# Routing logits taken from rows before their normalisation, and the order of loads around the first expert block

## The reference, cut to what matters

```
y = merged @ w_out
x = layer_norm(alpha * x + (1.0 + gt1) * y, ln_g[0], ln_b[0])
h = x * (1.0 + sc2) + sh2
p_grp  = softmax(h @ w_route_grp)             # 4 groups
logits = h @ w_route_exp                      # 32 experts, 8 in a group
# the best group, the two best experts in it, their gates
for each expert e:  hb = silu(xb @ w_gate[e]) * (xb @ w_up[e]);  yb = hb @ w_down[e]
x = layer_norm(alpha * x + (1.0 + gt2) * sum of gated yb, ln_g[1], ln_b[1])
```

## Time and profile before

| what | us |
|---|---|
| median of 3 runs (lowest, highest) | 2259.28 (2259.08, 2259.91) |
| the profiled execution's own time | 2261.59 |
| its span, first to last instruction | 2259.8 |
| TensorE busy | 2096.4 (93%) |
| VectorE busy | 1182.3 (52%) |
| ScalarE busy | 460.6 (20%) |

### The profile page before, as it was taken

One profiled execution on the slowest core, in us unless ns is written; L12 is line 12 of the kernel. 1 busy time (PEld: TensorE's weight loads), 2 busy tenths in 40 slices (PEclk: granted clock), 3 DMA queues, 4 the chain that ended last, 5 costly groups with the idle time before them and its releaser, 6 DMA issues.

```text
span 2259.8 us, 24654 instructions
## 1 busy us (share of the span) xinstructions
PE 2096.4 (93%) x9166; PEld 1344.4 (59%) x9166; DVE 1182.3 (52%) x2110; ACT 460.6 (20%) x948; POOL 132.2 (6%) x173
## 2 busy tenths in 40 slices
PE   8999898999999999998999999999996999999883
PEld 4444444888888845444788488888854433333331
DVE  2785654666677543367787467676446221121114
ACT  2215541100100010225211455410110000000003
POOL 1000000000000000000000043300000000010000
PEclk9999898999999999999999999999996999999996
DMA  7136600622122132221122000042445899999995
GB/s 260 61 118 239 221 1 1 158 75 90 60 103 103 56 100 75 75 75 38 38 75 88 24 2 1 2 152 75 168 168 233 348 423 426 426 427 426 426 401 221
DMA packets 97677, 364.71 MB, mean 161 GB/s; under 512 B 9340, under 2 KB 17969, under 8 KB 85521
## 3 DMA queue, kind: packets, MB, share of 16 engines
q1 hardware_dynamic: 88065, 340.62, 39.2%
q0 software_dynamic: 9392, 22.37, 2.8%
q10 hardware_dynamic: 96, 0.08, 0.0%
HBM read 357.00 MB, written 17.57 MB: 166 GB/s over the span
## 4 chain that ended last, share of the span: by engine, by line
PE 79%; DVE 12%; DMA 5%; issue 2%; ACT 2%; SPq 0%; DVEq 0%; ACTq 0%; POOLq 0%
PE bank L752 52%; PE bank L1552 9%; PE bank L1545 6%; PE bank L818 3%; DMA mem<-in_w_gate 2%; DMA mem<-in_w_up 2%; PE bank L1235 2%; PE bank L993 2%; PE bank L863 1%; PE bank L1526 1%; DVE mem L2166 1%; DVE mem L1669 1%; DVE mem L1664 1%; DVE mem L1668 1%; DVE mem L1665 1%
## 5 line engine op out<-in xcount | busy, mean ns | idle before, releaser
L752 PE MATMUL bank<-mem 128*128 128x256 f32 (+7 forms) x5032 | 1348.7, 430 | 24.1 <-ACT mem L2584 11.0
L752 PEld LDWEIGHTS bank<-mem 128*128 128x128 f32 (+2 forms) x5032 | 932.9, 192 | 392.2 <-issue 264.5
L1552 PE MATMUL bank<-mem 128*64 128x512 f32 x1184 | 269.3, 610 | 28.2 <-DMA mem<-in_w_gate 9.9
L1552 PEld LDWEIGHTS bank<-mem 128*64 128x64 f32 x1184 | 88.3, 140 | 198.9 <-issue 184.4
L2584 ACT ACTIVATE mem<-bank 128x512 f32<-128x512 f32 (+4 forms) x277 | 140.1, 506 | 325.0 <-PE bank L752 152.1
L818 PE MATMUL bank<-mem 128*128 128x128 f32 (+1 forms) x740 | 124.6, 302 | 39.1 <-DVE mem L1824 15.2
L2520 DVE TENSOR_TENSOR mem<-mem,bank 128x512 f32<-128x512 f32 x19 | 13.1, 690 | 268.6 <-PE bank L1552 171.0
L818 PEld LDWEIGHTS bank<-mem 128*128 128x128 f32 (+1 forms) x740 | 92.2, 152 | 95.3 <-DVE mem L1824 40.1
L1545 PE MATMUL bank<-mem 128*128 128x512 f32 x288 | 127.0, 596 | 4.1 <-ACT mem L2900 4.1
L2718 ACT ACTIVATE mem<-bank 128x512 f32<-128x512 f32 (+1 forms) x62 | 36.3, 585 | 459.8 <-PE bank L752 458.1
L1545 PEld LDWEIGHTS bank<-mem 128*128 128x128 f32 x288 | 53.5, 189 | 73.7 <-issue 68.4
(11 more groups left out here) (364 smaller groups left out, 1716.9 us busy)
## 6 DMA issues: line engine op xcount, KB each, us to landing
mem<-in_w_gate SPq DMA_DIRECT2D x37, 2048.0 KB, 23.3
mem<-in_w_up SPq DMA_DIRECT2D x35, 2048.0 KB, 25.2
mem<-in_w_down SPq DMA_DIRECT2D x34, 2048.0 KB, 26.7
mem<-in_w_in SPq DMA_DIRECT2D x18, 2048.0 KB, 8.0
mem<-in_w_ada SPq DMA_DIRECT2D x12, 2048.0 KB, 8.0
mem<-in_w_out SPq DMA_DIRECT2D x4, 2048.0 KB, 14.0
mem<-in_w_ple_gate SPq DMA_DIRECT2D x2, 2048.0 KB, 7.8
mem<-in_w_br_att SPq DMA_DIRECT2D x2, 2048.0 KB, 7.7
```

Source lines behind the costliest of these rows:

```text
L752: last = pe.matmul(o, l, r, start=(i == 0), stop=(i == len(pairs) - 1))
L1552: last_ = pe.matmul(o[here, :], lhs[:, k, here], w[:, k, cols], start=(k == 0), stop=(k == kk - 1))
```

## The change

Four things are changed, all between the mixer and the second expert block.

1. The rows are turned before they are normalised (`rows_turned`, as soon as `row_added` says that both halves are added), VectorE copies them plainly into `hT` (`rows_taken`), and the logits are made with weights that hold the gain and the scale (`w_by_row`, columns 0 to 35). A product of ones with `w_by_row` (`route_constants`, 72 columns) gives the sums that mean and shift need; `logits_taken` puts the two together in two small instructions, with the mean and the deviation that the normalisation has anyway. For this, gain and shift are loaded once more by column, and VectorE makes `w_by_row` before the output stage. The rows are still normalised and written to memory as before, but nothing of the logits waits for the long instructions.
2. The output products are taken by half tiles in a new order, with turns and logits products between them; two more small products stand ahead of the last one.
3. `all_slots` stands behind the gate product of block 0 and no longer in its middle; a gate product waits for the first half of its turned rows only, and in its middle for the second. The reduction into `place_of` stands behind the first `slots_from`.
4. Load 7 waits for the row writes, as load 8 does.

```diff
@@ -435,6 +435,9 @@
         flat_T = xgT.rearrange("p a b c -> p (a b c)")
+        route_rows, logit_sum = flat_T[:, 512:584], flat_T[:, 584:620]
+        w_by_row = place(M0 + 3 * D + KD * 36, KD, 72)
+        route_cols = choice_all[:, 0, 0, 0:2 * KD].rearrange("p (j k) -> p j k", j=2)
...
@@ -484,6 +487,7 @@
         x_spilled = sem("x_rows_written")
+        row_added = sem("out2_added_to_row")
...
@@ -1451,17 +1455,19 @@
 
-            def out2_rows(q):
-                for c in range(2):
-                    if q == 0 and c == 1:
-                        pe.wait_ge(fast_read, 5 * N_FAST)
-                    b = bank("dve")
-                    full(product(b[:, :], [(S5["mg"][:, k, q * P:(q + 1) * P], out2[c][:, k, :])
-                                           for k in range(KD)]), "dve")
-            def normal_rows_turned(q):
+            def out2_rows(q, c):
+                if q == 0 and c == 1:
+                    pe.wait_ge(fast_read, 5 * N_FAST)
+                b = bank("dve")
+                full(product(b[:, :], [(S5["mg"][:, k, q * P:(q + 1) * P], out2[c][:, k, :])
+                                       for k in range(KD)]), "dve")
+            def route_constants():
                 to_wait(to_pe)
-                mark["x normalised", q] = nxt[to_pe]
+                full(product(bank("dve")[:, 0:72], [(const("ones"), w_by_row[:, k, :]) for k in range(KD)]), "dve")
+            def rows_turned(q):
+                pe.wait_ge(row_added, q + 1)
...
@@ -1469,28 +1475,35 @@
                 pe.wait_ge(dve_free, turned_at[q])
-                full(product(b[:, 0:36], [(hT[:, k, q * P:(q + 1) * P], w_route[:, k, :]) for k in range(KD)]), "dve")
+                full(product(b[:, 0:36], [(hT[:, k, q * P:(q + 1) * P], w_by_row[:, k, 0:36]) for k in range(KD)]), "dve")
...
             assert done["dve"] % 4
-            out2_rows(0)
+            out2_rows(0, 0)
+            out2_rows(0, 1)
             pe.wait_ge(mixed_ready, 2)
-            out2_rows(1)
-            normal_rows_turned(0)
-            pe.wait_ge(route_loaded, 32)
-            out2_rows(2)
-            normal_rows_turned(1)
+            out2_rows(1, 0)
+            rows_turned(0)
+            out2_rows(1, 1)
+            out2_rows(2, 0)
+            rows_turned(1)
+            route_constants()
             routed_rows(0)
-            out2_rows(3)
+            out2_rows(2, 1)
+            out2_rows(3, 0)
+            rows_turned(2)
+            routed_rows(1)
+            out2_rows(3, 1)
...
             used("dve")
-            normal_rows_turned(2)
-            routed_rows(1)
             routed_rows(2)
-            normal_rows_turned(3)
-            mark["x normalised"] = nxt[to_pe]
+            rows_turned(3)
...
             routed_rows(3)
+            for q in range(NT):
+                nxt[to_pe] += 1
+                mark["x normalised", q] = nxt[to_pe]
+            mark["x normalised"] = nxt[to_pe]
...
@@ -1582,10 +1595,12 @@
 
-                pe.wait_ge(xt_taken, 2 * n + 2)
+                pe.wait_ge(xt_taken, 2 * n + 1)
...
                 expert_product(banks[2][:, :], xgT[:, n % 2, :, :], weights_here(n, "gate", wide_at), every, KD,
-                               all_slots if n == 0 else None).then_inc(gate_full, 1)
+                               lambda: pe.wait_ge(xt_taken, 2 * n + 2)).then_inc(gate_full, 1)
+                if n == 0:
+                    all_slots()
...
@@ -2364,6 +2379,12 @@
             V(dve.memset(ln_eps_col, LN_EPS))
+            dve.wait_ge(route_loaded, 64)
+            V(tt(route_cols, route_cols, mod[:, 3:4, :].to_broadcast([P, 2, KD]), ALU.mult))
+            V(tt(route_cols[:, 1, :], route_cols[:, 1, :], mod[:, 2, :], ALU.add))
+            for j in range(2):
+                V(tt(w_by_row[:, :, 36 * j:36 * j + 36], w_route, inner(route_cols[:, j, :], 36), ALU.mult),
+                  to_pe if j else None)
...
@@ -2374,39 +2395,48 @@
             dve.wait_ge(x_again, 16)
-            def out2_added(q):
-                for c in range(2):
-                    o = x[:, q, c * 512:(c + 1) * 512]
-                    V(tt(S5["tmp"], take()[:, :], gate_rows[:, 0, c * 512:(c + 1) * 512], ALU.mult), dve_free)
-                    V(stt(o, o, ALPHA, S5["tmp"], ALU.mult, ALU.add), var_ready if c else None)
+            def out2_added(q, c):
+                o = x[:, q, c * 512:(c + 1) * 512]
+                V(tt(S5["tmp"], take()[:, :], gate_rows[:, 0, c * 512:(c + 1) * 512], ALU.mult), dve_free)
+                V(stt(o, o, ALPHA, S5["tmp"], ALU.mult, ALU.add), row_added if c else None)
...
 
+            def rows_taken(q):
+                for hf in range(2):
+                    V(dve.tensor_copy(hT[:, 4 * hf:4 * hf + 4, q * P:(q + 1) * P],
+                                      take()[:, :].rearrange("p (a b) -> p a b", a=4)), dve_free)
             def logits_taken(q):
-                V(dve.tensor_copy(logit[:, q, :], take()[:, 0:36]), dve_free)
+                V(stt(logit_sum, route_rows[:, 0:36], stat[:, q:q + 1], take()[:, 0:36], ALU.mult, ALU.add), dve_free)
+                V(stt(logit[:, q, :], logit_sum, stat[:, 4 + q:5 + q], route_rows[:, 36:72], ALU.mult, ALU.add))
...
             V(dve.memset(both_and_none[:, NT, :], 0.0))
-            out2_added(0)
+            out2_added(0, 0)
+            out2_added(0, 1)
+            out2_added(1, 0)
+            rows_taken(0)
             ln1(0)
-            out2_added(1)
-            turned_in(0, mod[:, 3, :], mod[:, 2, :])
+            out2_added(1, 1)
+            out2_added(2, 0)
+            rows_taken(1)
+            V(dve.tensor_copy(route_rows, take()[:, 0:72]), dve_free)
             ln1(1)
-            out2_added(2)
-            turned_in(1, mod[:, 3, :], mod[:, 2, :])
+            logits_taken(0)
+            out2_added(2, 1)
+            out2_added(3, 0)
+            rows_taken(2)
             ln1(2)
-            logits_taken(0)
-            out2_added(3)
-            turned_in(2, mod[:, 3, :], mod[:, 2, :])
             logits_taken(1)
+            out2_added(3, 1)
+            logits_taken(2)
+            rows_taken(3)
             ln1(3)
-            logits_taken(2)
-            turned_in(3, mod[:, 3, :], mod[:, 2, :])
             logits_taken(3)
...
@@ -2441,7 +2471,6 @@
             V(tt(pairs_of, over(key, EXPERTS), inner(key, EXPERTS), ALU.is_gt))
-            V(dve.tensor_reduce(place_of, pairs_of, AX.X, ALU.add))
...
@@ -2449,6 +2478,7 @@
             slots_from(take()[:, 0:1], SEQUENCE[0], SEQUENCE[0] + 1, dve_free)
+            V(dve.tensor_reduce(place_of, pairs_of, AX.X, ALU.add))
...
@@ -2572,9 +2602,9 @@
 
-            def spread_of(q, junk):
-                wait_next(var_ready)
+            def spread_of(q, junk, ready=var_ready):
+                wait_next(ready)
...
@@ -2886,7 +2916,7 @@
             for q in range(NT):
-                spread_of(q, ln1_junk)
+                spread_of(q, ln1_junk, row_added)
...
@@ -2984,6 +3014,9 @@
             pool.dma_start(w_route[:, :, 4:36], w3(W["w_route_exp_2"])).then_inc(route_loaded, 16)
+            for j, name in enumerate(("ln_g_2", "ln_b_2")):
+                pool.dma_start(route_cols[:, j, :], bass.AP(tensor=t[name].tensor, offset=0, ap=[[1, P], [P, KD]]),
+                               allow_slow_non_contiguous=True).then_inc(route_loaded, 16)
...
@@ -3073,7 +3106,7 @@
                           item_done[len(items) - 2], item_done[len(items) - 1], item_done[len(items) - 1],
-                          (to_pe, mark["x normalised"]), (x_spilled, 16 * NT), (dve_full, mark["routed"])]
+                          (x_spilled, 16 * NT), (x_spilled, 16 * NT), (dve_full, mark["routed"])]
...
```

## The result

| | before | after |
|---|---|---|
| median of 6 runs each, us | 2259.18 | 2267.9 |
| lowest and highest | 2257.39, 2260.88 | 2259.89, 2269.14 |
| profiled execution, its own time | 2261.59 | 2269.14 |
| its span | 2259.8 | 2267.3 |

The changed kernel is slower: ratio 1.003, with a 95% interval of 1.002 to 1.004, that is 4.5 to 9 us. The forecast was 2266.0.

A forecast was written before the change was run, and what follows sets the result against it. It took the expert-weight stream, full from 1763 us on, to bound the kernel: TensorE late by 0.7 + 5.1 + 1.7 = 7.5 us, less 0.8 of room, so 2259.3 + 6.7 = 2266.0 us; range 2256 to 2270.

The forecast's parts named there:

- (a): Case that both gathers meet the expert-weight loads and take 10.7 us each; 2263.5 to 2269.5 us, chance 46%.
- first gate product starts, against before: First expert block: gather lands 2.6 us later, half-tile start saves 0.5 and 1.4, so 0.7 us later.
- load 10, against before: Start of the weight stream: first gate product, without the slots' 1.97 us, ends 1.2 us earlier, load 10 too.
- TensorE stands: Before block 1's turns: second gather lands 23.3 us after gate product start, wanted at 18.2; TensorE waits 5.1 us.
- slower clock behind it: After TensorE's wait: next product partly at the lower clock, 8.74 us in place of 7.10, +1.7.
- room: At the third gate product: TensorE can be only 0.8 us later before the weight stream has a hole.
- Output stage and routing chain: Output products to first gather: logits 3.6 us earlier, moved reduction wins 1.1, gather issued at 1737.2; new weight work hidden.
- The meeting with the loads: First gather goes out 1.2 us behind loads 7 and 8, takes 10.7 us instead of 3.4, lands 2.6 later.
- the row write's company: Last row write: loads 4, 5 and 6 stay in flight though load 7 is held; 11.3 us against 2.9 alone.
- the trace agrees: Gather under load: 10.7 us lies inside the 9.0 to 14.0 estimated from the skill's packet-by-packet queue rule.
- The slots: Slots behind first gate product: second gather issued 12.6 us after its start, behind loads 10 and 11, taking 10.7.
- no longer matters: After the load released by the third gate product, the queue fills up and TensorE's lateness has no effect.

The follow-up runs named there:

- e2: Changed kernel, but load 7 goes out with the last normalised row block and load 8 waits for the first gather to land; 2262.99 us (before 2259.88).
- e8: Changed kernel reduced to the output stage and the moved reduction: load 7 early, slots in mid gate product, both halves awaited; 2261.49 us (before 2261.23).
- e1: Changed kernel with the slot table's product back in the middle of the first gate product; 2260.66 us (before 2259.88).
- e4: Kernel before with only the slot table's product moved behind the first gate product; 2266.48 us (before 2259.88).
- e9: Changed kernel plus five unused TensorE products while it would stand for the second gather; 2265.32 us (before 2260.35).
- e6: Changed kernel with only load 7's new wait taken back, so it goes out with the last normalised row block; 2268.29 us (before 2261.23).
- e5: As e2, and load 10 and all behind it wait until the second gather has landed; 2260.98 us (before 2261.23).

## Why the prediction was right

The likeliest case was (a), and it is what happened: both gathers met the loads. Its steps, in us from the first output tile:

| step | forecast | measured |
|---|---|---|
| loads 4 and 5 issued | 56.0 | 56.1 |
| last logits | 64.0 | 63.9 |
| first gather issued | 76.0 | 75.9 |
| first gather, issue to landing | 10.7 | 10.7 |
| first gate product starts, against before | +0.7 | +0.6 |
| load 10, against before | -1.2 | -1.9 |
| second gather issued, after start of the gate product | 12.6 | 12.0 |
| TensorE stands | 5.1 | 4.8 |
| slower clock behind it | 1.7 | 3.5 |
| third gate product, against before | +7.5 | +8.5 |
| room | 0.8 | 1.1 |
| last 2 MB load landed, against before | +6.7 | +7.4 |
| end, against before | +6.7 | +6.5 |

**Output stage and routing chain.** Right, and free of surprise: the three small products, the plain copies (1.42 us for two), the two small operations and the reduction behind the first slots came out within 0.2 us. The new work on the weights was hidden: behind it VectorE still stood 2.4 us for the first output tile.

**The meeting with the loads.** Right. e2 and e8 show it from both sides: with one load less ahead of it the gather takes 5.5 us, with the output stage alone 10.6. That the row write's company is not removed by holding load 7 was right as well (10.7 us held, 10.4 to 11.6 in the runs that didn't hold it).

How the gather is held up is seen in the records of the DMA packets. The gather has 144 packets, nine for each of the 16 DMA engines if they are spread evenly. In the kernel before they all start 1.6 to 3.1 us after the issue of their gather. In the changed kernel the second gather's packets start 4.2 to 10.0 us after its issue. Of the 144, 138 start within 0.012 us of the end of a 16 KB piece of a load, and 119 are followed by the next piece at once. For 1769.5 to 1771.5 the DMA view counts nearly as many of one queue as of the other (q0 the gather, q1 the loads):

```profile
q1 hardware_dynamic: 52, 0.85, 99.4%
q0 software_dynamic: 51, 0.02, 3.8%
```

So the two queues take turns piece by piece, and as an estimate from these records nine packets behind one piece of 0.61 us each are 5.5 us. Why the first comes only after 4.2 us is not shown. The estimate from the Trainium skill ("DMA: Bandwidth & Descriptors", "Queues, rings and completion order"), 9 to 14 us if the gather waits while an engine drains 9 to 17 pieces of a load, covers the 10.4 to 11.0 us of the first two gathers where they met a running stream (the later ones took 8.3 to 12.1). But the trace doesn't bear out the way in which it comes about: here it was one piece and then the other queue's turn. The times lie in the range and don't confirm the rule, and the prediction's "the trace agrees" said too much.

**The slots.** Right in place and size, and it is the cause: e1 and e4 take the one edit out of the change and put it alone into the kernel before, and the loss goes and comes with it.

**Terms were mis-sized, and they cancel.** The slower clock costs 3.5 us (3.5 also by e9) where the prediction took the 1.7 of a shorter stand: the clock was down for all of the turns (0.8 us more), for those of the hidden rows (0.4) and for most of the down product (2.3), not for one piece. The room was 1.1 us and not 0.8: load 19 was issued 8.5 us late, found 0.4 us in its queue (8.5 - 8.1), and the last 2 MB load landed 7.4 late. In between, TensorE gives nothing back: loads 20 to 81 are all issued 8.4 to 8.6 us late. That it "no longer matters" there was right, for these loads take up to 41 us from issue to landing, so the queue is never empty. The rest comes behind the last load, and no term of the sum stood for it (the chains that ended last, before and after):

```profile
2155.99 41.10 DMA mem<-in_w_gate
...
2197.23 8.79 PE bank L1552 x32
```

```profile
2167.23 38.23 DMA mem<-in_w_gate
...
2205.61 7.10 PE bank L1565 x32
```

The last gate product ran at the slower clock before and at the faster one after, which takes 1.7 us off; behind it 0.8 is lost again, and by what is not shown. e6 has the same 7.10 and the same gain there. e2, e4 and e9 have 8.79 as before, and their ends are as late as their last loads to within 0.4 us. The clock of that one product is in no term of the prediction, so that its end agrees to 0.2 us is partly luck; the mechanism and its two large steps, the stand and the late gathers, are not.

**The medians** differ by 8.7 us, the spans by 7.5, and from the first output tile by 6.5. The profile's own difference of 1.0 lies ahead of the stage. The rest up to 8.7 is within the interval of 4.5 to 9 us.

## What to carry to other kernels

A small transfer that releases work must be looked at together with what goes out just ahead of it: here a gather issued 1 to 2.5 us behind 2 MB loads took 10.4 to 11.0 us, and one issued ahead of them 3.1 to 3.5. When a wait is moved so that big loads start sooner, ask which small gather now goes out behind them; a product of 2 us was moved off the way of the loads, and the kernel lost three times its length (e4). And where one engine's stream is full to the end, the end is the later of its start and of the releases that feed it: e5 had TensorE 4.6 us early and gained nothing, e2 had the stream 6 us early and lost.

## What the runs showed of the hardware

A gather of one block's rows took 3.1 to 3.5 us with the DMA engines free, 5.4 to 5.7 with the tail of one 2 MB load beside it, and 10.4 to 11.0 beside a running stream (8.3 to 12.1 for the later blocks). Its packets and the 16 KB pieces of the loads went through the DMA engines in turn, one and one (138 of 144 packets started at the end of a piece). A stand of TensorE of 4.8 us was followed by products at the lower clock (granted clock 0.60 from 1770 to 1780) that cost 3.5 us, nearly as much as the stand; five products without use in its place kept the clock up (granted clock 1.00 from 1760 to 1790 in e9).
